# A hybrid encoder step: attention heads normalized on ScalarE, gates stored in pairs, the final norm in three parts

## The reference

```python
xn = rms_norm(x, norm_mix_g)
a_q, a_k, a_v, a_qi, a_ki, a_w, f_q, f_k, f_v, f_f = split(xn @ w_in)
o_a = dsa_attention(...)   # indexer scores, top 256 keys, 8 query heads on 2 key heads
o_f = fox_attention(...)   # 8 heads, causal, cumulative log-forget bias
h = x + concat(o_a, o_f) @ w_out
h = h + memory_attention(rms_norm(h, norm_mem_g), ...)      # 4 heads, 256 memory rows
h = h + peer_ffn(rms_norm(h, norm_ffn_g), ...)              # 16384 experts, below
y = rms_norm(h, final_norm_g)

def peer_ffn(xn, w_q, keys1, keys2, u, v):      # per token, 8 heads
    s1, s2 = products of the two query halves with 128 keys each
    v1, i1 = top_k(s1, 16);  v2, i2 = top_k(s2, 16)
    sv, si = top_k(v1[:, None] + v2[None, :], 16);  eidx = i1 * 128 + i2 at si
    g = softmax(sv);  h = gelu(xn . u[eidx])
    return sum of g * h * v[eidx]
```

## Time and profile before

| | us |
|---|---|
| median of 3 runs | 4098.74 |
| lowest, highest | 4086.96, 4101.52 |
| profiled execution, its own time | 4097.7 |
| its span, first to last instruction | 4095.9 |
| TensorE, VectorE, ScalarE, GpSimd busy in it | 3492.9, 2424.6, 1031.4, 1940.9 |

### The profile page before, as it was taken

One profiled execution on the slowest core, in us unless ns is written; L12 is line 12 of the kernel. 1 busy time (PEld: TensorE's weight loads), 2 busy tenths in 40 slices (PEclk: granted clock), 3 DMA queues, 4 the chain that ended last, 5 costly groups with the idle time before them and its releaser, 6 DMA issues. The chain is left out here.

```text
span 4095.9 us, 50522 instructions
## 1 busy us (share of the span) xinstructions
PE 3492.9 (85%) x17237; PEld 2519.8 (62%) x17237; DVE 2424.6 (59%) x5921; ACT 1031.4 (25%) x1848; POOL 1940.9 (47%) x1478
## 2 busy tenths in 40 slices
PE   7887888898978977877898889868579999999996
PEld 4445566667778866655676767655356556565554
DVE  3778885342222366779999998998533333333334
ACT  1213334341121222221232222223222222122221
POOL 0000000003214333777887878855367776676761
PEclk9889999898998999888999999989889999999998
DMA  2001000004303444789999999969999999999983
GB/s 113 10 32 34 17 12 6 10 0 146 108 26 129 139 138 163 281 323 348 383 395 376 388 376 395 381 242 382 338 353 339 365 356 351 355 363 357 368 337 143
DMA packets 370009, 960.30 MB, mean 234 GB/s; under 512 B 33680, under 2 KB 119576, under 8 KB 368256
## 3 DMA queue, kind: packets, MB, share of 16 engines
q0 software_dynamic: 156672, 570.49, 36.3%
q1 hardware_dynamic: 207184, 369.60, 25.5%
q10 hardware_dynamic: 5936, 17.44, 1.2%
HBM read 862.73 MB, written 94.68 MB: 234 GB/s over the span
## 5 line engine op out<-in xcount | busy, mean ns | idle before, releaser
L1535 PE MATMUL m_ps<-m_xh_flat,m_wh 128*128 128x512 f32 x3072 | 759.7, 405 | 145.4 <-POOL m_wh L1525 143.5
L2467 PE MATMUL e_y_ps<-e_wh,e_vh 128*128 128x512 f32 x3072 | 743.6, 398 | 50.3 <-DVE e_wh L2585 42.4
L1535 PEld LDWEIGHTS m_ps<-m_xh_flat,m_wh 128*128 128x128 f32 x3072 | 588.0, 195 | 311.5 <-POOL m_wh L1525 186.3
L2467 PEld LDWEIGHTS e_y_ps<-e_wh,e_vh 128*128 128x128 f32 x3072 | 570.5, 189 | 268.6 <-issue 113.4
L981 POOL CAST m_wh<-m_w 128x1024 fp32r<-128x1024 f32 x40 | 42.6, 1064 | 1204.5 <-issue 937.3
L1018 PE MATMUL m_ps<-m_xh_flat,m_wh 128*128 128x272 f32 (+1 forms) x2880 | 500.7, 335 | 66.8 <-DVE m_xh_flat L1074 20.1
L1018 PEld LDWEIGHTS m_ps<-m_xh_flat,m_wh 128*128 128x128 f32 x2880 | 439.8, 196 | 122.3 <-issue 42.6
L2176 POOL DMA_INDIRECT e_rows<-in_v,eid x448 | 435.0, 971 | 119.8 <-issue 106.5
L2620 DVE TENSOR_TENSOR oT<-e_y_ps,oT 128x512 f32<-128x512 f32 x256 | 175.5, 686 | 502.5 <-PE e_y_ps L2467 502.5
L2545 POOL TENSOR_TENSOR e_vh<-e_v,e_vh 128x1024 fp32r<-128x1024 f32 x128 | 306.6, 2396 | 234.6 <-ACT e_vh L2490 233.2
L1525 POOL TENSOR_TENSOR m_wh<-m_w,m_wh 128x1024 fp32r<-128x1024 f32 x128 | 306.9, 2397 | 55.6 <-ACT m_wh L1520 53.4
(11 more groups left out here) (298 smaller groups left out, 5233.2 us busy)
## 6 DMA issues: line engine op xcount, KB each, us to landing
m_w<-in_ut SPq DMA_DIRECT2D x128, 512.0 KB, 5.6
e_v<-in_v SPq DMA_DIRECT2D x124, 512.0 KB, 7.3
s_hid<-flat SPq DMA_DIRECT2D x128, 256.0 KB, 7.0
e_hid<-s_hid SPq DMA_DIRECT2D x124, 256.0 KB, 6.1
e_gate<-s_gate SPq DMA_DIRECT2D x124, 256.0 KB, 6.8
s_gate<-g_stage SPq DMA_DIRECT2D x3, 8192.0 KB, 72.1
m_w<-in_w_pq SPq DMA_DIRECT2D x32, 512.0 KB, 3.8
m_w<-in_w_out SPq DMA_DIRECT2D x16, 512.0 KB, 3.7
```

The lines of the kernel that those rows point to most:

```text
L1535: mm = pe.matmul(self.ps[:, n % 2, 0:ND], self.uh[:, at % 2, a, k * P:(k + 1) * P], self.xd[:, b, k, :], start=(k == 0 and o == 0), stop=( ...
L2467: mm = pe.matmul(y_ps[:, o, 0:TD], vh[:, n % SLOT, a, m * P:(m + 1) * P], wh[:, SLOT - 1 - n % SLOT, b, g * TD:(g + 1) * TD], start=(c == ...
```

## The change

It has five parts. (1) In both attention stages the normalization moves from VectorE to ScalarE: an activation with the reciprocal as scale, written two units later. VectorE's reciprocal keeps its wait for the normalization two units back. (2) In the gate stage s_gate has one row for two experts, so a store writes 256 floats in a run where it wrote 128; the table sum_after moves the sparse sums; v and hid of the first two expert blocks are loaded already here. For that their buffers, `w` and `xrow`, live on from the stages before. (3) In the expert stage the gates come in pairs, 512 KB a load, all on SP, into e_gate and the joined buffer gh; the first two pairs are loaded ahead of everything else. (4) slot_of spreads the steps up to number 136 over the slots and puts the last four behind the loop. (5) The final norm is in three parts: columns 0 to 511 in the middle of the last phase, the dense columns after it, and the 32 of the sample at the end.

```diff
+                def normalize(u):
+                    t, e = UNITS[u]
+                    M = rows_of(t)
+                    act.wait_ge(pv_ready, j * NU + u + 3)
+                    act.wait_ge(o_inv, j * NU + u + 3)
+                    if e == 0:
+                        act.wait_ge(x_ready, j * QT + max(t + 1, 2))
+                    act.activation(opair[0:M, t % 2, e * HD:(e + 1) * HD], o_ps[0:M, u % 2, 0:HD], ACT.Copy,
+                                   scale=rinv[0:M, u % 2:u % 2 + 1]).then_inc(o_normed, 1)
                 for u, (t, e) in enumerate(UNITS):
                     M = rows_of(t)
+                    if u >= 2:
+                        normalize(u - 2)
                     if u + 1 < NU:
                         exponentials(u + 1)
...
-                    if u >= 1:
-                        dve.wait_ge(o_inv, j * NU + u + 2)
-                        normalize(u - 1)
...
-        TURN_AT, FIRST = 3, 20
-        sum_after = [FIRST + b * (NB * NQ - FIRST) // B_STEPS for b in range(B_STEPS)]
+        TURN_AT = 3
+        sum_after = [8 + 4 * b if b < 8 else NQ + 8 + (b - 8) * 14 // 3 for b in range(B_STEPS)]
...
-                sp.dma_start(dram["s_gate"][:, :, n * TB:(n + 1) * TB].rearrange("a p t -> p a t"),
-                             stage[:, 1 - n % 2]).then_inc(stored[n % 2], 16)
+                sp.dma_start(dram["s_gate"][:, :, 2 * n * TB:2 * (n + 1) * TB].rearrange("a p t -> p a t"),
+                             pairs(1 - n % 2)).then_inc(stored[n % 2], 16)
+                if n < 2:
+                    sp.dma_start(keep["w"][:, n, :], dram["v"][n]).then_inc(keep["v_ready"][n], 16)
+                    sp.dma_start(keep["xrow"][:, n * ND:(n + 1) * ND], dram["s_hid"][n]).then_inc(keep["hid_ready"][n], 16)
...
-    return C_FIRST + (s - B_STEPS) * (C_LAST - C_FIRST) // (N_STEP - 1 - B_STEPS)
+    return C_FIRST + (s - B_STEPS) * (C_LAST - C_FIRST) // (LAST_IN - B_STEPS) if s <= LAST_IN else N_SLOT
...
+        norm_r = final_norm(0, C0, hid, sums.ps[:, 1, 0:1, :])
+        norm_d = final_norm(NSP, NT, v[:, :, 0:ND], sums.ps[:, 1, 1:2, :])
+        norm_s = final_norm(C0, NSP, gate, y_ps[:, 0:1, :])
...
+            for m in range(CG // 2):
+                load_gates(sp, m)
             for n in range(CG, NKEY):
                 load_v(sp, n)
                 load_hid(sp, n)
-                load_gate(sp, n)
+                if n % 2 == 0:
+                    load_gates(sp, n // 2)
...
-            act.wait_ge(sum_added, 2 * (NS + 1))
-            norm.act(act, lambda k: (y_added, (NPH - 1) * NY + (k + 1) * NGD))
+            act.wait_ge(w_split, NKEY)
+            norm_r.act(act, lambda k: (sum_added, 2 * NS))
+            act.wait_ge(v_split, NKEY)
+            norm_d.act(act, lambda k: (y_added, (NPH - 1) * NY + (k + 1) * NGD))
+            keep_sum(NS)
+            norm_s.act(act, lambda k: (sum_added, 2 * (NS + 1)))
...
-                dve.tensor_tensor(hid[:, n % 2, :], hid[:, n % 2, :], gate[:, n % 2, :], ALU.mult).then_inc(weighed, 1)
+                dve.tensor_tensor(by_batch(hid[:, n % 2, :]), by_batch(hid[:, n % 2, :]), gates(n), ALU.mult).then_inc(weighed, 1)
```

More of the change, by code:

```diff
@@ L783, in _ @@
                         tile_out(act, j, t - 1)
+                for u in range(NU - 2, NU):
+                    normalize(u)
                 tile_out(act, j, QT - 1)
@@ L2224, in spread_gates, with pairs @@
         stage = ctx.enter_context(nc.sbuf_tensor("g_stage", [P, 2, NKEY, TB], F32))
+        def pairs(b):
+            return stage[:, b].rearrange("p (a i) t -> p a (i t)", i=2)
         hot1 = ctx.enter_context(nc.sbuf_tensor("g_hot1", [P, 4, 4, NKEY], F32))
@@ L2377, in experts @@
         gate = sb("gate", [P, 2, ND])
-        hid = sb("hid", [P, 2, ND])
+        pair = (gate[:, :, :].rearrange("p a n -> p (a n)"), keep["gh"][:, 0:2 * ND])
+        v, hid = keep["w"], keep["xrow"][:, :].rearrange("p (a n) -> p a n", a=2)
         rows = sb("rows", [P, NBUF, D])
@@ L2426, in _ @@
                 load_hid(sp, n)
-                load_gate(sp, n)
-            for g in range(NG):
-                sp.wait_ge(norm.normed, norm.ready(g))
-                cols = slice(g * TG, (g + 1) * TG)
-                sp.dma_start(dram["o_y"][:, :, cols], y[:, :, cols]).then_inc(stored, 16)
-            sp.wait_ge(stored, 16 * NG)
+                if n % 2 == 0:
+                    load_gates(sp, n // 2)
+            for norm, a, b in ((norm_r, 0, C0), (norm_d, NSP, NT), (norm_s, C0, NSP)):
+                sp.wait_ge(norm.normed, norm.all)
+                sp.dma_start(dram["o_y"][:, :, a:b], y[:, :, a:b]).then_inc(stored, 16)
+            sp.wait_ge(stored, 48)
         @block.tensor
@@ L2455, in _ @@
                 for b0 in range(0, NY, 4):
+                    if p == NPH - 1 and b0 == NY - 4:
+                        pe.wait_ge(set_, 1)
+                        norm_r.pe(pe)
                     for c in range(CG):
@@ L2478, in _ @@
                                 sparse_sum(batch_at(s))
+            norm_d.pe(pe)
+            for s in range(LAST_IN + 1, N_STEP - 1):
+                sparse_sum(batch_at(s))
+            turn_sum(NS)
             pe.wait_ge(y_added, NPH * NY)
-            pe.wait_ge(set_, 1)
-            norm.pe(pe)
+            norm_s.pe(pe)
         @block.scalar
@@ L2498, in round_w, with keep_sum @@
                 act.activation(wh[:, SLOT - 1 - n % SLOT, HI, :], hid[:, n % 2, :], ACT.Copy).then_inc(w_rounded, 1)
-            for n in range(2):
-                load_v(act, n)
-                load_hid(act, n)
+            def keep_sum(t):
+                act.wait_ge(sums.summed, LAST_OF[t] + 1)
+                if t > 0:
+                    act.wait_ge(sum_turned, t)
+                act.activation(ysp[:, :], sums.ps[:, t % 2].rearrange("p a b -> p (a b)"), ACT.Copy).then_inc(sum_copied, 1)
             for n in range(2):
@@ L2606, in _ @@
                     n = (p + 1) * CG + i
+                    if p == NPH - 1 and i == 2:
+                        dve.wait_ge(loaded, 16)
+                        norm_r.dve(dve)
                     for o in range(2 * i, 2 * i + 2):
@@ L2625, in _ @@
             dve.wait_ge(y_added, NPH * NY)
+            norm_d.dve(dve)
+            add_sum(NS)
             dve.wait_ge(sum_added, 2 * (NS + 1))
-            dve.wait_ge(loaded, 16)
-            norm.dve(dve)
+            norm_s.dve(dve)
 def build(nc, dram):
@@ L2667, in build @@
             attention_pairs(nc, mix_sem, dram, keep, False)
+        keep["w"] = ctx.enter_context(nc.sbuf_tensor("raw", [P, 2, D], F32))
+        keep["xrow"] = ctx.enter_context(nc.sbuf_tensor("xrow", [P, D], F32))
+        keep["v_ready"], keep["hid_ready"] = ([sem(f"e_{n}{c}_ready") for c in range(2)] for n in ("v", "h"))
         with nc.sbuf_tensor("routes", [P, 3, NT], F32) as routes:
```

61 lines of the change are left out of this document (24 added, 37 removed).

## The result

The changed kernel took 4068.3 us (median of 4 runs, 4065.3 to 4078.3) against 4099.8 for the kernel before on the same chip: ratio 0.9926, 95% interval 0.9909 to 0.9944. Faster by 31 us (0.7%), half of what was forecast. The profiled execution took 4069.5 us, with a span of 4067.7 against 4095.9.

A forecast was written before the change was run, and what follows sets the result against it. The prediction held that no single engine bounds the kernel; its terms, -18 + 0 - 10 - 8 - 5 - 10 - 11 = -62, took the profiled 4097.7 us to 4036, range 4012 to 4066.

The forecast's parts named there:

- FoX pairs, -18: FoX heads: normalization leaving VectorE saves 18 us over four pairs (13.0 durations, 7.2 idle time); bounds 13 and 22.
- Rival A: FoX pairs: TensorE becomes the longer chain, -4 instead of -18, total 4050; chance 0.12.
- Rival C: Attention units: ScalarE, queued behind values(u-2), delivers each exponential late, +93 replaces -18, total 4147; chance 0.04.
- Sparse pairs, 0: Sparse-attention heads: removing normalizations from VectorE frees nothing, as it idles 41.4 us before them; bounds -4 to +6.
- Gate stage, -10: Gate stage: 1 KB store pieces shorten two stalls, -8; sparse sums moved earlier, -2; bounds 0 and -20.
- rival D: Gate stores: small pieces already run at full rate, gate stage -2, start -4, total 4048; chance 0.11.
- Start, -8 and -5: Into the expert loop: last store issue to first product 30.3 us, -8; first phase -5 with gates already there.
- the last sign that the forecast named for being wrong: Start of the expert stage: a gate load lands only after long waits behind the stores.
- Tail, -11: Last phase to end: norm in parts, 60 us instead of 70.8, saving 11; bounds -5 to -16.
- The loop, -10: Expert loop, 30 phases: three sums moved behind it, -8.9, and larger gate loads, 1; bounds -4 and -20.
- B: Expert loop: DMA alone decides, -20 there, total 4026; chance 0.14.
- E: Whole kernel: parts exist but give under a third, each freeing a resource beside the waiting one, 4080; chance 0.03.

The follow-up runs named there:

- single gates: Changed kernel with gates stored and loaded expert by expert as before (512 B store pieces, 256 KB loads): 4064.5 us, ratio 0.9890.
- gathers-first kernels: GpSimd's gathers issued ahead of its split of v: in the kernel before, 4003.2 us; in the changed kernel with gates one by one, 3965.4 us.

## Why the prediction was half right

**FoX pairs, -18: right, in part by luck.** It was -20.5. From the first reciprocal to the last, the time for which normalizations held VectorE was 13.7 us against 13.0 worked out. But the idle time of 7.2 us in the earlier trace rows mostly moved: VectorE now waits 3.4 us before its reciprocals and 2.7 us more before its row maxima, so only 1 us of it was won. The other 5.7 us came from a stand that the forecast did not price. At the end of a pair VectorE used to stand about 2 us before it scaled f_k (it is in the earlier trace rows); after the change that stand is gone. Why is not shown. Before (310 to 643 us) and after (308 to 621 us):

```profile
L813 DVE TENSOR_SCALAR f_k<-gb,con 40x1184 f32<-40x1184 f32 x6 | 4.8, 836 | 5.8 <-issue 5.8
...
L828 DVE TENSOR_SCALAR f_k<-gb,con 40x1184 f32<-40x1184 f32 x6 | 4.8, 837 | 0.1
```

Rival A, TensorE as the longer chain from -4 on, is refuted: between SyncE's landmarks the periods are 88.0, 85.9 and 85.3 us (92.1, 92.0 and 91.9 before). Rival C too: exponentials do not wait for anything new, and ScalarE's idle time before them in the FoX phase fell from 93.5 to 61.4 us. **Sparse pairs, 0: right**, under 1 us.

**Gate stage, -10: right in sum, wrong in one part.** It was -10.8 between the two profiles, -8 over all executions, and with single gates nothing. The pieces give it; the 2 us given to the earlier sums are not there. ScalarE's wait fell from 35.9 to 16.4 us, more than the forecast's 27 (14.6 and 24.0 in two other executions with 1 KB pieces), and with the stores alone the wider pieces run at 343 GB/s where the earlier trace rows have 288:

```profile
2910.00:2923.00 13.00, 0.00 (x0) 0.00 (x0) 0.00 (x0) 0.00 (x0) 0.00 (x0) 0.57 1.04 343
```

That refutes rival D, by which halving the number of pieces gives nothing. The Trainium skill, "DMA: Bandwidth & Descriptors", section Specifications, puts full rate at 512 B and above; here single gates and pairs disagree with that, 236.2 against 224.8 us for the same bytes, and the measurement decides.

**Start, -8 and -5: right in kind, a quarter short.** Store to product 32.6 us against 30.3 worked out, and -2.8 for phase 1, whose length scatters from 43.8 to 49.6 us in the kernels with the old start. The gate load, which I priced at 1.3 us behind the store, landed 15.2 us after its issue, in the queue behind that store, which is the last sign that the forecast named for being wrong:

```profile
2923.64 5.53 SPq L2433 DMA_DIRECT2D e_gate<-s_gate  x1
...
2938.87 1.29 DVE L2611 TENSOR_TENSOR xrow<-xrow,e_gate 128x512 f32<-128x512 f32 x2 [14.95 <-DMA e_gate<-s_gate]
...
2941.09 4.18 PE L2493 MATMUL e_y_ps<-e_wh,e_vh 128*128 128x512 f32 x9 [33.22 <-DVE e_wh L2616]
```

**Tail, -11: right, 3 us mis-sized.** From TensorE's last phase to the end 62.8 us against 60. The marks I gave were 18.7 for the first mean squares, 29.9 for the last products, 50.5 for the dense normalization; the rows give 20.4, 31.8 and 51.7. I had left out the sum of 1.92 us that stands between the first 48 products and the mean squares; the rest is the last small norm. The rows answer to the earlier trace rows:

```profile
4004.94 11.22 PE L2493 MATMUL e_y_ps<-e_wh,e_vh 128*128 128x512 f32 x48
...
4016.09 1.92 PE L2209 MATMUL z_ps<-e_rows,flat 128*32 128x512 f32 x16
4017.94 7.98 PE L149 MATMUL z_ps<-xrow,e_ones 128*128 128x512 f32 x16
...
4025.36 11.50 PE L2493 MATMUL e_y_ps<-e_wh,e_vh 128*128 128x512 f32 x48
...
4036.69 7.60 PE L149 MATMUL z_ps<-raw,e_ones 128*128 128x512 f32 x16
...
4051.37 5.39 DVE L180 SCALAR_TENSOR_TENSOR oT<-oT,e_gain,raw 128x512 f32<-128x512 f32 x8
```

**The loop, -10: this is the step that failed, in sign.** It had two faults. The first: "Gate loads change from 16384 pieces of 2 KB to 8192 of 4 KB ... of which I count 1" priced the pair by its bytes and passed over its place. On SyncE's queue v of the odd expert now stands behind 256 KB more; v lands at a median of 8.0 us instead of 7.3; ScalarE rounds it later; GpSimd's split waits 207 us instead of 171; the gathers behind it are later; TensorE waits longer and works more of its time at half clock. The times of v, of GpSimd's wait and of TensorE's are in the rows; which causes which, the experiments show. Load order alone brings the loop to 1001 to 1006 us. Distance of the gathers (907.8) and order of GpSimd (904.8) take away TensorE's waits for rows with v as late as in the changed kernel (8.4 and 8.0 us), and then the pair costs 5.7 us instead of 21. Only the part of the half clock is an association: spells followed waits, but not each wait. The second fault: 2.97 us as the price of a sum, 1.05 of it waiting. That waiting goes away with the order on GpSimd, the number of sums unchanged, so it does not belong to the sum, and taking a sum away takes about 2 us: 4.9 for three sums put back, 8.9 between the two gathers-first kernels with four fewer sums and single gates, 1.6 and 2.2 each.

How large is it, chance apart? Six executions with the loop of before gave 1000.5 to 1016.0, mean 1009.0; two of the changed kernel 1022.3 and 1023.0. So the change costs the loop about 14 us. The three variants with gates in another order average 1003.5: the place of the pair costs 19, and the fewer sums with all else give back 5.5. Between the two profiles compared at first, 3 of the 17 us were chance.

**The middle, 0: unforeseen and not settled.** In five executions with the old places of the raw buffers the middle took 1766.6 to 1770.9 us, mean 1768.9; in thirteen with the new places 1766.5 to 1777.2, mean 1773.1. A cost of some 4 us is likely, but it is missing in some executions, and which place would cause it was not tried.

By parts the miss of 34 us of span (28.2 against 62) is 27 for the loop, 6 for the middle, 2 each for phase 1 and the start, 3 for the tail, less 5 won in attention and 1 at the gates. The loop's failure was no rival of mine: B had it faster, E was a guess without a mechanism.

## What to carry to other kernels

When a load grows or moves on a queue, price its place as well as its bytes: name what stands behind it and follow that to the engine that waits, in-order queue by in-order queue. When an engine that issues gathers also computes, put the gathers ahead of what can stall, or issue them a step sooner; here that was worth 97 us, three times the whole change, and it showed in a row of before (170.7 us of idle time on GpSimd) that a busy share of 0.94 on DMA made look harmless. And a resource that looks full need not be the bound: with rows on time the same DMA engines moved 390 GB/s for the kernel before instead of 353, and 385 for the changed one instead of 340.
